# Head means of the first block's keys and queries: one fp32 multiplication, or two one-pass multiplications of a rounded part and a rest

## The chip, the cores and the metric

The kernel runs on one core of a Trainium2 chip. The metric is the device time of one execution in microseconds (us). Three runs of the kernel before took 2369.74 to 2370.86 us, with a median of 2370.79 us.

## The reference

The reference is a chain of two transformer blocks on 256 tokens of width 1024, each of depth 2, in float32. The first block also has 256 context tokens. In the second layer of the first block the context is only read, so queries there cover 256 columns and keys 512. Only one small step matters here. In the first block, queries and keys of two attention families (`na` with a neighbourhood window, `gqa` with grouped heads) are divided by their root mean square over each head of 64 features before they are used:

```
def rms_norm(x, gain=None):
    xf = x.astype(jnp.float32)
    y = xf * lax.rsqrt(jnp.mean(xf * xf, axis=-1, keepdims=True) + EPS)
...
na_q = lambda p: rms_norm(heads(p['na_q'], N_NA_HEADS, HEAD_DIM), na_q_norm)
na_k = lambda p: rms_norm(heads(p['na_k'], N_NA_HEADS, HEAD_DIM), na_k_norm)
gqa_q = lambda p: rms_norm(heads(p['gqa_q'], N_GQA_HEADS, HEAD_DIM), gqa_q_norm)
gqa_k = lambda p: rms_norm(heads(p['gqa_k'], N_GQA_KV_HEADS, HEAD_DIM), gqa_k_norm)
```

The same norm stands behind the gated linear attention (`gla`).

## The kernel before, in words

Activations are kept transposed: 128 features on the partitions, tokens on the free dimension (512 columns for both streams, 256 for the tokens alone). All weights stream from HBM in units of 128 x 1024. ScalarE (ACT) copies each unit, rounded to fp32r, into `ring_high` (L1390), VectorE (DVE) subtracts that from the unit and leaves the rest in `ring_low` (L1920), and TensorE (PE) multiplies in three one-pass products, high by high, high by low and low by high (L816 to L818). A unit is 8 chunks of three such products.

The mixing stage of a layer of the first block runs over steps k = 0 to 20, and each engine has its own written-out program for a step. Between engines there is nothing but semaphores: an engine executes its queue in order, and a wait holds up everything behind it.

- PE in step k: the scores of the attention tile that is due (L1140), pairs of the gated linear attention (L1192), the projection k (24 products, L816 to L818), then the head means that are due (`head_mean`, L1119), then transposes and attention values (L1079, L1158, L1170). Projections 0 to 3 are computed together beforehand; the means of items 0 and 1 are placed inside projection 4, after its fourth chunk, and the products for the gates (L1256) after its sixth.
- ACT in step k: copies of turned tiles (L1648), `qk_square` (L1591), the gates' exponentials (L1663, L1666), the decays (L1714), exponentials of scores (L1616, L1617), copies out of the projection (L1578) and the next unit's high part (L1390), then the root of the mean (`head_root`, L1397 and L1400).
- DVE in step k, in this order: the row maxima of the next attention tile (`maxima`, L2297 to L2316), the scaling by the root (`qk_norm`, L2243), rotary parts, low parts of attention results (L2350), in steps 4 to 6 the gates (`gla_log_gates` L2362 and L2365, `gla_sums` L2371 and L2380), from step 10 four masked copies (L2435), and then `project`: the copy out of projection k (L2218), normalised probabilities (L2334 to L2346) and the low part of a weight unit (L1920).

There are seven normed items in each layer: `NAK`, `NAQ`, `NAK+1`, `NAQ+1`, `GQAK`, `GQAQ`, `GQAQ+1`, numbered i = 0 to 6. Their means fall into steps 2, 2, 5, 7, 9, 10 and 12 (`means_at`). For each, ACT squares the 128 x n item into `squares` (two buffers), PE multiplies the squares by a constant 128 x 128 matrix that holds 1/64 in the two diagonal blocks (`C_ONES64`), ACT makes the reciprocal root and DVE scales the item. n is 512 for all items of the first layer and for the three keys of the second, and 256 for the four queries of the second. The multiplication is a plain fp32 one, which appears as two records in the trace. The gated linear attention has two more such means in each layer, at the end of the mixing.

Of the kernel before, what the change touches and what calls it, by code (L numbers as in the profile page):

```python
# [29 lines left out]
F32 = mybir.dt.float32  # L30
F32R = mybir.dt.float32r
I32 = mybir.dt.int32
ALU = mybir.AluOpType
# [3 lines left out]
P = 128  # L37
# [182 lines left out]
def build(nc, A, old=None):  # L220
    ev = Events(*(old or (None, None)))
    ctx = ExitStack()
    with ctx:
        top = [nc.sbuf_base + (-nc.sbuf_base) % 64]

        def sb(name, cols, dt=F32, over=None):

            if over is None:
                over = top[0] = -(-top[0] // 64) * 64
                top[0] += cols * mybir.dt.size(dt)  # L230
            place_of[name] = over
            return nc.alloc_sbuf_tensor_at(name, [P, cols], dt, offset=over)[:, :]
# [19 lines left out]
        def when(name, *key):  # L252

            if ev.counting:
                return high_parts, 1
            family, value = ev.known[(name, *key)]
            if family not in ev.sems:
                ev.sems[family] = sem(family)
            return ev.sems[family], value
# [59 lines left out]
        wgate = sb("wgate", DEPTH * 2 * P).rearrange("p (l n) -> p l n", l=DEPTH)  # L319
        squares = sb("squares", 2 * N1).rearrange("p (b n) -> p b n", b=2)  # L320
        sumsq = sb("sumsq", N1)
        rstd = sb("rstd", 2 * N1).rearrange("p (b n) -> p b n", b=2)
        act_out = sb("act_out", 2 * N1).rearrange("p (b n) -> p b n", b=2)
        c_wide = act_out[:, 0, 0:KC * 32].rearrange("p (c n) -> p c n", c=KC)
        fresh = sb("fresh", 2 * N1).rearrange("p (b n) -> p b n", b=2)
        zeros = fresh[:, 1, NX:N1]
        narrow = sb("narrow", N2 + 8 * NARROW)
        row_scale = narrow[:, 0:N2]
        gate_w = narrow[:, 16:16 + 16 * NARROW].rearrange("p (s b n) -> p s b n", s=2, b=8)
# [39 lines left out]
        def cst(at, n=P, rows=P):  # L369
            return const[0:rows, at:at + n]  # L370
# [412 lines left out]
        def _(pe):  # L783
# [3 lines left out]
            def take(*key):  # L787

                b = taken[0] % 8
                taken[0] += 1  # L790
                if b in bank_user:
                    pe.wait_ge(*when("free", *bank_user[b]))
                bank_user[b] = key
                ev.banks[key] = b
                return psum[b]
# [319 lines left out]
                mm.then_inc(*made("dft_l", l, s))  # L1115

            def head_mean(tag, i, n):
                pe.wait_ge(*when("head_squares", tag, i))
                pe.matmul(take("head_mean", tag, i)[:, 0:n], cst(C_ONES64),  # L1119
                          squares[:, i % 2, 0:n], start=True, stop=True).then_inc(*made("head_mean", tag, i))  # L1120

            def scores(pr, j):
                q0, nq, nk = pr["tiles"][j]
# [250 lines left out]
        def _(act):  # L1374
# [212 lines left out]
            def head_square(tag, i, ready, x, n):  # L1587
                act.wait_ge(*ready)
                if i >= 2:
                    act.wait_ge(*when("head_mean", tag, i - 2))  # L1590
                act.activation(squares[:, i % 2, 0:n], x, ACT.Square).then_inc(*made("head_squares", tag, i))  # L1591
# [8 lines left out]
            def qk_square(l, i):  # L1600
                tm, (slot, _, n) = ("mix1", l), norm_items(l)[i]
                head_square(tm, i, when("projected", tm, SLOT1[slot]), proj1[:, slot, 0:n], n)

            def exps(pr, j):
                q0, nq, nk = pr["tiles"][j]
# [303 lines left out]
        def _(dve):  # L1909
# [336 lines left out]
            def qk_norm(l, i):  # L2246
                slot, gain, n = norm_items(l)[i]
                head_norm(("mix1", l), i, proj1[:, slot, 0:n], scalar1(l, gain), n, "projected", ("mix1", l),
                          SLOT1[slot])

            def rope_sin(tag, i, sin, n):
                dve.wait_ge(*when("rotated", tag, i))
                if i >= 1:
                    dve.wait_ge(*when("roped", tag, i - 1))
                dve.tensor_tensor(fresh[:, 0, 0:n], bank("rotated", tag, i)[:, 0:n], sin, ALU.mult).then_inc(
                    *made("rope_sin", tag, i, frees=("rotated", tag, i)))
# [149 lines left out]
            def mixing(l):  # L2406
                tm, to = ("mix1", l), ("out1", l)
                n = N1 if l == 0 else NX
                ntile = n // P
                turns = first_tiles(l)  # L2410
                for k in range(MIX_STEPS):
                    if k + 1 in turns:
                        maxima(*turns[k + 1])
                    for i in means_at(l, k - 1):
                        if i not in root_first(l, k - 1):
                            qk_norm(l, i)
                    for i in means_at(l, k - 2):
                        if i >= 4:
                            rope(tm, i - 4, proj1[:, rope_items[i - 4], 0:NX], cst(C_COS1, NX), NX, "head_normed", tm, i)
                    for pr in owed_at(l, k - 1):  # L2420
                        mixed_low(pr)
                    if k == 4:
                        gla_log_gates(l)
                    if k == 5:
                        gla_sums(l, 0)
                    if k == 6:
                        gla_sums(l, 1)
                    if LEVEL_STEP + 1 <= k < LEVEL_STEP + LEVELS + 1:
                        v = k - LEVEL_STEP - 1
                        dve.wait_ge(*when("masks_loaded", 0))  # L2430
                        for h in range(4):
                            dve.wait_ge(*when("pairs", l, v, h))
                            p = bank("pairs", l, v, h)
                            dve.wait_ge(*(when("gla_scores", l, v - 1, h) if v else when("gla_first", l, h)))
                            dve.copy_predicated(gla_s[:, h, 0:ntile], masks[:, v:v + 1].broadcast_to([P, ntile, P]),  # L2435
                                                p[:, 0:n].rearrange("p (t n) -> p t n", n=P)).then_inc(
                                                    *made("gla_scores", l, v, h, frees=("pairs", l, v, h)))
                    if k < len(PROJ1):
                        project(tm, PROJ1, k, width1(l, PROJ1[k]), proj1, VTEMP1, turns.get(k + 1),
                                items=root_first(l, k), rotated=[i for i in means_at(l, k - 1) if i >= 4])  # L2440
                    elif k + 1 in turns:
                        normalise(*turns[k + 1])
                    if k == 6:
                        gla_z(l)
                    if k == LEVEL_STEP - 1:
                        gla_ends(l)
                    if k == LEVEL_STEP + LEVELS:
                        gla_starts(l)
                    s = k - LEVEL_STEP - LEVELS - 3
                    if 0 <= s < 2 - l:  # L2450
                        for c in range(2):
                            dve.wait_ge(*when("gla_out", l, s, c))
                            dve.tensor_copy(proj1[:, GLAQ + c, s * NX:(s + 1) * NX],
                                            bank("gla_out", l, s, c)[:, 0:NX]).then_inc(
                                                *made("gla_out_sb", l, s, c, frees=("gla_out", l, s, c)))
                    if k == len(PROJ1):
                        for s in range(2 - l):
                            dve.wait_ge(*when("dft_d", l, s, 0))
                            dve.tensor_copy(dft_ab[:, s, 0], bank("dft_d", l, s, 0)[:, 0:2 * P]).then_inc(
                                *made("dft_ab_dve", l, s, frees=("dft_d", l, s, 0)))  # L2460
                    if k == len(PROJ1) + 1:
                        hi, lo = x_parts(N1)
                        for s in range(2 - l):
                            if s == 1:
                                gla_finish(l)
                            at = slice(s * NX, (s + 1) * NX)
                            dve.wait_ge(*when("four_high", l, s))
                            dve.tensor_tensor(lo[:, 0:2, at], bank("dft_l", l, s).rearrange("p (g n) -> p g n", g=2),
                                              hi[:, 0:2, at].bitcast(F32), ALU.subtract).then_inc(
                                                  *made("four_low", l, s, frees=("dft_l", l, s)))  # L2470
                        for c in range(2):
                            ev.table[("x_low", to, c)] = ev.table[("four_low", l, 1 - l)]
                for pr in owed_at(l, MIX_STEPS - 1):
                    mixed_low(pr)
# [170 lines left out]
            for c in range(1, KC):  # L2645
# [3 lines left out]
                if c == 1:  # L2649
                    split_ahead(1)  # L2650
            split_ahead(1)
            for l in range(DEPTH):
                for name in ("naq", "gqaq"):
                    dve.tensor_scalar(scalar1(l, name), scalar1(l, name), HD ** -0.5, None, ALU.mult).then_inc(
                        *made("gain_scaled", l, name))
# [168 lines left out]
```

## Time and profile before

| what | value |
|---|---|
| median of 3 runs | 2370.79 us |
| profiled execution | 2369.99 us, span 2368.2 us |
| PE busy | 2348.6 us, 99% of the span |
| DVE, ACT, POOL busy | 65%, 43%, 17% |
| granted TensorE clock, mean | 0.999 |
| mixing, first layer | about 410 to 572 us |
| mixing, second layer | about 1359 to 1479 us |

The profiled execution is 1.8 us longer than its span and 0.8 us shorter than the median. Busy shares say which engine is nearly always at work, but matmuls overlap in the records (the next starts before the end of the last), so what one costs is read from the distance of starts. What a wait costs is read from the stretch in which it lies.

### The profile page before, as it was taken

The page shows a single profiled execution, that of the slowest core. Times are in us where ns is not written, and L with a number is a line of the kernel's source. Part 1 is how long each engine was busy: PE and PEld are TensorE (multiplying, and loading weights), DVE is VectorE, ACT ScalarE, POOL GpSimd, SP SyncE. Part 2 cuts the span into 40 slices and gives each one's busy share as a digit, 9 for nine tenths or more (in the row PEclk, how much of TensorE's full clock was granted, in tenths as well). Part 3 has the DMA queues.
Part 4 walks back from the last instruction along what each step waited for, and adds up shares of the span by engine and source line. Part 5 has one row for each costly group of instructions (what it writes and reads, how often), then busy time and mean ns, then how long its engine had stood idle before and what let it go on. Part 6 is the DMA issues. An engine that isn't in the chain of part 4 may idle for free.

```text
span 2368.2 us, 36508 instructions
## 1 busy us (share of the span) xinstructions
PE 2348.6 (99%) x14378; PEld 2039.4 (86%) x14378; DVE 1534.2 (65%) x2611; ACT 1017.9 (43%) x1734; POOL 405.8 (17%) x427
## 2 busy tenths in 40 slices
PE   9999999999999999999999999999999999999998
PEld 6888889777888888988888877999989999999887
DVE  5888775784698865523322576766677665667874
ACT  5222234654522223422223465545456444456663
POOL 2221221240122131111011121121000220000110
PEclk9999999999999999999999999999999999999999
DMA  9565542212366755222222222555534555434553
GB/s 355 195 209 206 182 159 89 66 55 98 114 212 238 247 207 178 89 98 98 98 94 95 81 99 82 173 184 187 172 118 142 173 175 176 156 120 162 190 188 134
DMA packets 97865, 360.76 MB, mean 152 GB/s; under 512 B 11024, under 2 KB 11792, under 8 KB 96544
## 3 DMA queue, kind: packets, MB, share of 16 engines
q1 hardware_dynamic: 75744, 272.84, 34.3%
q0 software_dynamic: 21952, 85.59, 10.1%
q8 instruction: 115, 1.88, 0.3%
q14 instruction: 54, 0.44, 0.1%
HBM read 357.34 MB, written 1.05 MB: 151 GB/s over the span
## 4 chain that ended last, share of the span: by engine, by line
PE 95%; DVE 1%; ACT 1%; issue 1%; DMA 1%; POOL 0%; DVEq 0%; ACTq 0%; POOLq 0%
PE bank L816 26%; PE bank L818 26%; PE bank L817 26%; PE bank L823 6%; PE bank L824 3%; PE bank L1170 1%; PE bank L1140 1%; PE bank L1158 1%; PE bank L1192 1%; DMA arena<-w_mod_first_dram 1%; PE bank L1119 0%; PE bank L1079 0%; ACT ring_high L1390 0%; PE bank L1344 0%; PE bank L1334 0%
## 5 line engine op out<-in xcount | busy, mean ns | idle before, releaser
L1920 DVE TENSOR_TENSOR ring_low<-ring,ring_high 128x1024 fp32r<-128x1024 f32 x520 | 641.1, 1233 | 484.4 <-ACT ring_high L1390 482.4
L816 PE MATMUL bank<-x_parts,ring_high 128*128 128x512 f32 (+2 forms) x2308 | 799.2, 346 | 2.3 <-POOL x_parts L637 1.4
L1390 ACT ACTIVATE ring_high<-ring 128x1024 fp32r<-128x1024 f32 x520 | 547.9, 1054 | 572.8 <-PE bank L818 528.8
L818 PE MATMUL bank<-x_parts,ring_low 128*128 128x512 f32 (+2 forms) x2308 | 786.3, 341 | 0.0
L817 PE MATMUL bank<-x_parts,ring_high 128*128 128x512 f32 (+2 forms) x2308 | 784.9, 340 | 0.0
L816 PEld LDWEIGHTS bank<-x_parts,ring_high 128*128 128x128 f32 x2308 | 434.6, 188 | 68.0 <-issue 13.2
L818 PEld LDWEIGHTS bank<-x_parts,ring_low 128*128 128x128 f32 x2308 | 434.6, 188 | 47.5
L817 PEld LDWEIGHTS bank<-x_parts,ring_high 128*128 128x128 f32 x2308 | 435.1, 189 | 46.9 <-issue 1.0
L647 POOL TENSOR_TENSOR hidden_parts<-fresh,hidden_parts 128x512 fp32r<-128x512 f32 (+2 forms) x132 | 203.4, 1541 | 1006.2 <-ACT hidden_parts L1523 1006.2
L1933 DVE CUSTOM_DVE_ANT_0 mod_products<-mod_ring,csilu 128x1024 bf16<-128x1024 f32 x224 | 303.1, 1388 | 30.3 <-DMA mod_ring<-w_mod_dram 28.7
L816 PE MATMUL bank<-hidden_parts,ring_high 128*128 128x512 f32 (+2 forms) x814 | 280.9, 345 | 0.2 <-POOL hidden_parts L647 0.2
L818 PE MATMUL bank<-hidden_parts,ring_low 128*128 128x512 f32 (+2 forms) x814 | 280.1, 344 | 0.0
L817 PE MATMUL bank<-hidden_parts,ring_high 128*128 128x512 f32 (+2 forms) x814 | 280.1, 344 | 0.0
L816 PEld LDWEIGHTS bank<-hidden_parts,ring_high 128*128 128x128 f32 x814 | 153.6, 189 | 18.8 <-POOL hidden_parts L647 0.6
L817 PEld LDWEIGHTS bank<-hidden_parts,ring_high 128*128 128x128 f32 x814 | 153.6, 189 | 18.2
L818 PEld LDWEIGHTS bank<-hidden_parts,ring_low 128*128 128x128 f32 x814 | 153.5, 189 | 18.0
L1512 ACT ACTIVATE act_out<-bank 128x512 f32<-128x512 f32 x66 | 39.5, 599 | 264.4 <-PE bank L818 260.0
L823 PE MATMUL bank<-x_parts,ring_high 128*128 128x512 f32 x352 | 123.2, 393 | 0.0
L823 PE MATMUL bank<-hidden_parts,ring_high 128*128 128x512 f32 x308 | 106.9, 392 | 0.0
L816 PE MATMUL bank<-early_parts,ring_high 128*128 128x258 f32 x352 | 99.9, 284 | 0.0
L818 PE MATMUL bank<-early_parts,ring_low 128*128 128x258 f32 x352 | 99.3, 282 | 0.0
L817 PE MATMUL bank<-early_parts,ring_high 128*128 128x258 f32 x352 | 99.3, 282 | 0.0
(268 smaller groups left out, 2756.8 us busy)
## 6 DMA issues: line engine op xcount, KB each, us to landing
ring<-stream_dram SPq DMA_DIRECT2D x517, 512.0 KB, 3.4
mod_ring<-w_mod_dram POOLq DMA_DIRECT2D x128, 512.0 KB, 4.4
arena<-w_mod_first_dram POOLq DMA_DIRECT2D x8, 1024.0 KB, 11.7
ring<-stream_dram POOLq DMA_DIRECT2D x3, 512.0 KB, 10.8
arena<-na_bias_dram POOLq DMA_DIRECT2D x2, 768.0 KB, 11.8
mod_ring<-consts_dram POOLq DMA_DIRECT2D x1, 1076.0 KB, 5.3
resid<-x_dram POOLq DMA_DIRECT2D x2, 512.0 KB, 6.0
resid<-ctx_dram POOLq DMA_DIRECT2D x2, 512.0 KB, 7.2
```

Of the source, the lines that this page charges most:

```text
L647: pool.tensor_tensor(lo[:, f], fresh[:, f % 2, 0:n], hi[:, f].bitcast(F32), ALU.subtract).then_inc(*made("hidden_low", tag, h, f))
L816: pe.matmul(out, w[0][:, b], xh, start=start, stop=False)
L817: pe.matmul(out, w[0][:, b], xl, start=False, stop=False)
L818: return pe.matmul(out, w[1][:, b], xh, start=False, stop=stop)
L823: pe.matmul(bank.rearrange("p (k n) -> p k n", k=2), w[0][:, b], both, start=start, stop=False)
L824: return pe.matmul(bank[:, 0:NX], w[1][:, b], high, start=False, stop=stop)
L1140: mm = pe.matmul(out, pr["q"][r, q:q + nq], pr["k"][r, 0:NZ if twin else nk], start=not fox, stop=True, skip_group_check=nq < P)
L1158: mm = pe.transpose(p[0:rows, kt * P:kt * P + nq], probs[0:nq, b, e, kt * P:kt * P + rows], cst(C_IDENT, nq, nq))
L1390: act.activation(high[:, i % SPLIT], ring[:, u % LOADED], ACT.Copy).then_inc(high_parts, 1)
L1512: act.activation(act_out[:, f % 2, 0:n], p[:, 0:n], ACT.Silu).then_inc(*made("silu", tag, h, f, frees=("gate", tag, h, f)))
L1920: dve.tensor_tensor(low[:, u % LOADED], ring[:, u % LOADED], high_f[:, i % SPLIT], ALU.subtract).then_inc(low_parts, 1)
L1933: dve.tensor_tensor_reduce(junk[:, s], mod_ring[:, n % MOD_RING], csilu[:, s], 1.0, 0.0, ALU.mult, ALU.add, mod[:, l, s, j:j + 1]).then_in ...
```

## The change

The two gated means stay as they were. For the seven query and key items of each layer, ACT makes after the square a second pass, a copy rounded to fp32r (`square_high`); DVE subtracts it from the square and leaves the rest, as fp32r, in the place of the square (`squares_low`, a new step `square_low`); PE multiplies both by the constant matrix in fp32r, adding up in one bank, and now waits for `square_low` where it waited for the square. The rounded part lies in the place of `sumsq`, for item 1 in `fresh`. The constant matrix is rewritten once in its place as fp32r at the start (one DVE copy, `ones64`). `square_low` stands on DVE just ahead of `project` in step k, behind everything else of the step.

```
+            def square_low(l, i):
+                tm, n = ("mix1", l), norm_items(l)[i][2]
+                dve.wait_ge(*when("x_high", tm, "head", i))
+                dve.tensor_tensor(squares_low[:, i % 2, 0:n], squares[:, i % 2, 0:n],
+                                  square_high_of(i)[:, 0:n].bitcast(F32), ALU.subtract).then_inc(
+                                      *made("x_low_dve", tm, "head", i))
...
             def qk_square(l, i):
...
+                if i >= 2:
+                    act.wait_ge(*when("head_mean", tm, i - 1 if i > 2 else 0))
+                act.wait_ge(*when("head_squares", tm, i))
+                act.activation(square_high_of(i)[:, 0:n], squares[:, i % 2, 0:n], ACT.Copy).then_inc(
+                    *made("x_high", tm, "head", i))
...
             def head_mean(tag, i, n):
+                if tag[0] == "gla":
...
+                p = take("head_mean", tag, i)
+                pe.wait_ge(*when("ones64"))
+                pe.wait_ge(*when("x_low_dve", tag, "head", i))
+                pe.matmul(p[:, 0:n], ones64, square_high_of(i)[:, 0:n], start=True, stop=False)
+                pe.matmul(p[:, 0:n], ones64, squares_low[:, i % 2, 0:n], start=False, stop=True).then_inc(
+                    *made("head_mean", tag, i))
...
+                    for i in means_at(l, k):
+                        square_low(l, i)
                     if k < len(PROJ1):
                         project(tm, PROJ1, k, width1(l, PROJ1[k]), proj1, VTEMP1, turns.get(k + 1),
...
+            dve.wait_ge(*when("consts_loaded_rest", 0))
+            dve.tensor_copy(ones64, cst(C_ONES64)).then_inc(*made("ones64"))
```

## Rows read from the trace of the kernel before

**Rows 1.** The page: the chain that ended last, shares of the span by engine.
```profile
PE 95%; DVE 1%; ACT 1%; issue 1%; DMA 1%; POOL 0%; DVEq 0%; ACTq 0%; POOLq 0%
```

**Rows 2.** The chain in order of time, 400 to 440 us: start, us, what.
```profile
416.81 1.72 PE bank L1119 x4
418.52 0.23 PE bank L816
```

**Rows 3.** Timeline of PE, second layer, step 7: start us, us, engine, line, operation.
```profile
1389.00 0.28 PE L818 MATMUL bank<-x_parts,ring_low 128*128 128x256 f32 x1
1389.12 0.60 PE L1119 MATMUL bank<-squares,const 128*128 128x256 f32 x2
1389.78 0.39 PE L817 MATMUL bank<-x_parts,ring_high 128*128 128x512 f32 x1
```

**Rows 4.** Timelines of ACT and DVE: durations of passes like the added ones.
```profile
572.37 1.14 ACT L1423 ACTIVATE x_parts<-arena 128x512 fp32r<-128x512 f32 x2
573.57 1.28 DVE L1970 TENSOR_TENSOR x_parts<-arena,x_parts 128x512 fp32r<-128x512 f32 x2
1482.33 0.99 DVE L1970 TENSOR_TENSOR x_parts<-arena,x_parts 128x256 fp32r<-128x256 f32 x2
```

**Rows 5.** Timelines around items 0 and 1, one row of layer one, three of two.
```profile
417.70 0.69 ACT L1397 ACTIVATE rstd<-bank,eps_one 128x512 f32<-128x512 f32 x1 [1.13 <-PE bank L1119]
...
1363.77 0.92 ACT L1591 ACTIVATE squares<-arena 128x512 f32<-128x512 f32 x2
...
1368.95 1.30 DVE L2243 SCALAR_TENSOR_TENSOR arena<-arena,small,rstd 128x512 f32<-128x512 f32 x2
...
1371.56 1.13 PE L1140 MATMUL bank<-arena 64*128 64x512 f32 x4
```

**Rows 6.** Timeline of DVE, first layer, step 5.
```profile
429.78 0.42 DVE L2297 CUSTOM_DVE_ANT_0 arena<-bank,arena 128x256 f32<-128x256 f32 x1
...
432.17 1.27 DVE L2380 TENSOR_TENSOR_SCAN mod_ring<-eps_one,mod_ring 128x256 f32<-128x256 f32 x2
433.36 0.13 DVE L2334 TENSOR_TENSOR softmax_stats<-softmax_stats 128x1 f32<-128x1 f32 x1
```

**Rows 7.** Timelines of ACT and PE, first layer, step 5.
```profile
428.51 0.61 ACT L1591 ACTIVATE squares<-arena 128x512 f32<-128x512 f32 x1
429.57 1.02 PE L1119 MATMUL bank<-squares,const 128*128 128x512 f32 x2
```

**Rows 8.** Timelines of DVE and PE, second layer, step 5 and the waits behind it.
```profile
1378.61 1.13 PE L1119 MATMUL bank<-squares,const 128*128 128x512 f32 x2 [0.24 <-ACT squares L1591]
...
1381.60 1.27 DVE L2380 TENSOR_TENSOR_SCAN mod_ring<-eps_one,mod_ring 128x256 f32<-128x256 f32 x2
1382.79 0.13 DVE L2334 TENSOR_TENSOR softmax_stats<-softmax_stats 128x1 f32<-128x1 f32 x1
...
1383.35 0.66 PE L1079 MATMUL bank<-const,arena 128*128 128x128 f32 x4 [0.75 <-ACT arena L1578]
...
1398.78 1.95 PE L1170 MATMUL bank<-arena 128*64 128x256 f32 x16 [0.99 <-ACT arena L1648]
```

**Rows 9.** Timelines: DVE in steps 12, 7 and 12, PE in step 12.
```profile
491.93 0.69 DVE L2218 TENSOR_SCALAR arena<-bank 128x512 f32<-128x512 f32 x1 [0.37 <-PE bank L818]
...
1391.82 0.40 DVE L2316 TENSOR_SCALAR softmax_stats<-softmax_stats 128x1 f32<-128x1 f32 x2
...
1425.18 1.44 DVE L2435 COPY_PREDICATED gla_scores<-masks,bank 128x256 f32<-128x256 int32 x4
...
1425.39 0.60 PE L1119 MATMUL bank<-squares,const 128*128 128x256 f32 x2
```

**Rows 10.** PE's first records; stretches at the end (length, busy by engine, PEclk, DMA).
```profile
1.19 5.06 PE L914 MATMUL bank<-fresh 128*128 128x256 f32 x11 [1.19 <-DVE fresh L2592]
...
2357.00:2359.00 2.00, 1.77 (x15) 1.57 (x14) 0.19 (x1) 0.00 (x0) 0.00 (x0) 1.00 0.00 0
...
2361.00:2362.00 1.00, 0.00 (x0) 0.00 (x0) 0.11 (x1) 0.82 (x2) 0.00 (x0) 0.73 0.00 0
```

More of the change, by code:

```diff
@@ L321, in build @@
         sumsq = sb("sumsq", N1)
+        squares_low = sb("squares_low", 2 * N1, F32R, over=place_of["squares"]).rearrange("p (b n) -> p b n", b=2)
+        ones64 = sb("ones64", 2 + P, F32R, over=place_of["const"] + 4 * (C_ONES64 - 2))[:, 2:2 + P]
+        square_high = sb("square_high", N1, F32R, over=place_of["sumsq"])
         rstd = sb("rstd", 2 * N1).rearrange("p (b n) -> p b n", b=2)
@@ L326, in build, with square_high_of @@
         zeros = fresh[:, 1, NX:N1]
+        square_high1 = sb("square_high1", N1, F32R, over=place_of["fresh"] + 4 * N1)
+        def square_high_of(i):
+            return square_high1 if i == 1 else square_high
         narrow = sb("narrow", N2 + 8 * NARROW)
@@ L1117, in head_mean @@
             def head_mean(tag, i, n):
-                pe.wait_ge(*when("head_squares", tag, i))
-                pe.matmul(take("head_mean", tag, i)[:, 0:n], cst(C_ONES64),
-                          squares[:, i % 2, 0:n], start=True, stop=True).then_inc(*made("head_mean", tag, i))
+                if tag[0] == "gla":
+                    pe.wait_ge(*when("head_squares", tag, i))
+                    pe.matmul(take("head_mean", tag, i)[:, 0:n], ones64.bitcast(F32),
+                              squares[:, i % 2, 0:n], start=True, stop=True).then_inc(*made("head_mean", tag, i))
+                    return
+                p = take("head_mean", tag, i)
[4 more added lines that the diff above has]
+                    *made("head_mean", tag, i))
             def scores(pr, j):
```

## The prediction, made before the changed kernel ran

> **What bounds the kernel now.** I read the chain of waits on the page first, then the chain in order of time in the two mixing stages, then the timelines of PE, DVE and ACT there. TensorE carries 95% of the chain [rows 1]: what PE saves in a stage is saved in the time, and what PE waits is lost, unless the stage is one of the few that other engines pace. Inside the first layer's mixing the chain is PE alone; in the second layer, between 1363 and 1399 us, it runs over ACT and DVE, and PE waits for them at the marked places [rows 8]. So the question is how near each of the 14 means stands to the end of its square, now that an ACT pass and a DVE pass come between.
>
> **What PE saves.** Two fp32 means of 512 columns take 1.72 us, so one takes 0.86 [rows 2]. A one-pass product of 512 columns takes 0.23 [rows 2], and the new mean has two: 0.46. Saving 0.40. With 256 columns: from the start of the mean to the second product behind it 0.66 us, less one 0.23 product, is 0.43; a one-pass product of 256 is 0.12 (1389.00 to 1389.12), two are 0.24; saving 0.19 [rows 3]. There are ten means with 512 columns and four with 256: 4.0 + 0.8 = 4.8 us, if PE never waits.
>
> **What is added beside it.** ACT: 14 copies, 0.57 to 0.60 us for 512 columns. DVE: 14 subtractions, 0.64 for 512 columns, and at most 0.5 for 256 (the two in the row have a short wait between them; I take 0.4) [rows 4]. Both read SBUF and write SBUF like the rows they are priced from. The copy at the start, 128 x 128, is below a 128 x 256 pass and DVE idles there; it lies ahead of the first hidden chunk, which waits for PE; I take nothing, at most 0.3 us. The new waits of ACT for earlier means cost nothing: ACT has by then waited for those means in `head_root`.
>
> **Items 0 and 1.** The four ACT passes and two subtractions now stand ahead of the copy out of the gate projection, which ACT waits for before it goes on. In the second layer the squares start at 1363.77 [rows 5]; square, copy, square, copy end at 1365.73, the second subtraction at 1366.15, and everything behind on DVE and ACT is 1.07 us late. PE has its means at about 1365.8, nearly in time, saves 0.6, but its scores of step 5 need item 1 scaled, which ended at 1370.25 [rows 5] and now ends at 1371.3. PE would be there at 1371.0. So 0.25 of the 0.6 us stays. In the first layer ACT had 1.13 us of idle ahead of the root [rows 5], which takes part of the delay: DVE and ACT run some 0.75 us late, item 1 is scaled just in time, and PE keeps 0.8.
>
> **Item 2, the term that decides.** Its subtraction stands in step 5 behind the row maxima and `gla_sums` of that step. In the first layer DVE starts the maxima at 429.78, ends the scans of `gla_sums` at 433.44 and only then comes to `project` (433.36 is its first instruction there) [rows 6]. PE starts the mean at 429.57, just behind the square, which ended at 429.12 [rows 7]. DVE being some 0.75 us late, the subtraction runs from 434.1 to 434.75. PE, 0.8 us early, would start at 428.8 and stands still until 434.8: 6.0 us. In the second layer the scans end at 1382.87 [rows 8]; 1.07 us late, that is 1383.9, and the subtraction is ready at 1384.55. PE was there at 1378.2 (the mean waited 0.24 for its square and started at 1378.61) [rows 8], now at 1377.95: it waits 6.6 us, and the mean ends 5.55 us later than before. Queued behind it on PE is everything of the stage. In the second layer two old waits go, because ACT and DVE catch up meanwhile: about 0.9 us ahead of L1079 (0.75 by the releaser) and 0.99 ahead of L1170 [rows 8]. Bounds for each wait: below, the subtraction as soon as the copy is there (2 us in the first layer); above, one DVE pass of 1.3 us later than I have it.
>
> **The other means.** Second layer, step 7: the maxima end at 1392.22 on DVE [rows 9] and the mean started at 1389.12 [rows 3]. DVE is 1.7 us late by then, PE 4.6: wait 0.6 us. Second layer, step 12: the masked copies ended at 1426.62, the mean started at 1425.39 [rows 9], so the subtraction is ready at 1427.0: wait 1.6 us. DVE is here in step with PE, whose scores it waited for, so a late PE doesn't help. First layer, step 12: DVE had 0.37 us to spare [rows 9] and now needs 0.65: 0.5 us with the semaphore. The rest (steps 7, 9 and 10 of the first layer, 9 and 10 of the second) have DVE in front of PE by more than the pass, and PE simply gains.
>
> **Sum at full clock.** First layer: -0.8 + (6.0 - 0.4) - 3 x 0.4 + (0.5 - 0.4) = +3.7. Second layer: +5.55 (with items 0 and 1 in it), -0.9, +0.6 - 0.2, -1.0, -0.4, -0.2, +1.6 - 0.2 = +4.85. Together +8.5 us.
>
> **The clock.** A wait of 6 us is longer than any inside the kernel before. At its end PE stops its dense products about 2358.8, does two short matmuls, and the granted clock, 1.00 until then, averages 0.73 in the microsecond from 2361 [rows 10]: it went from 2.4 to 1.2 GHz less than 3 us after the products stopped. At the start, PE's first eleven fp32 records of 256 columns begin at 1.19 and 5.06 us hold them, 0.44 apart [rows 10], against 0.43 / 2 = 0.22 for such a record later [rows 3]: PE worked some 4.4 us at the low level before it rose. Half of that time, 2.2 us, is what one fall can cost; nothing is the other end, as shorter waits inside the kernel show no fall. I take 1.8 for each of the two waits, nearer the upper end because the row at the end shows the fall; the 0.6 us wait of step 7 in the second layer then goes. That is +3.0, and +11.5 in all.
>
> The Trainium skill ("TensorE: Matmul & The Clock Gate", "HAM oscillation — how this bites in real kernels") says that a matmul loop that lets the array idle while it waits finds the half clock when it goes on, and pays for the ramp at each such wait. The end of this trace agrees (0.73 in the microsecond from 2361); by the rule both waits pay, without it the sum would stay at +8.5.
>
> From the profiled execution's 2369.99 us this gives 2381.5. The median lies 0.8 higher, so I forecast 2382 us.
>
> **Rivals.**
> - *The clock holds.* For it: nothing inside the kernel before fell. Against: no wait there was this long, and the end of the trace fell sooner. 2370.8 + 8.5 = 2379 us.
> - *Longer low clock, or later waits that I hold for hidden* (steps 7 and 9, where DVE is ahead by about a microsecond): both falls at 2.2 us and two waits of 1 us more give 2385.
> - *The subtraction is in time* (the other side). If DVE came to step 5's subtraction 5 us earlier than the rows show, PE would save its 4.8 us, less the waits of steps 7 and 12 (2.7) and the 0.4 lost at items 0 and 1: 2369, no slower than before. For it speaks only that DVE idles elsewhere in the stage; against it that maxima and scans stand ahead of the subtraction in DVE's order and end 3.9 and 4.3 us after PE's start of the mean. It decides once the two waits of step 5 together are below 4 us.
> - *The one-pass means aren't cheaper*: 4.8 us of saving missing, 2386.5. Against it: the 0.23 and 0.12 us products in the rows are of this type.
>
> **How the numbers follow.** The forecast with the clock falling 0.58, the clock holding 0.2, the longer case 0.13, in time 0.05, no cheaper means 0.04. The bounds of the item 2 waits (2 to 7.5 us) and of the clock (0 to 2.2 each) and the neighbours give 2375 to 2387 us. About 0.2%, 4.7 us, is what a measurement of this kernel can tell from no change. Slower by more, above 2375.5: all cases but the one in time and a small part of the holding clock, 0.93. Within: 0.04. Faster, only if nearly all waits vanish: 0.03.
>
> **What would show it.** Right: the means of item 2 (fifth step of each layer) appear in PE's timeline with idle of about 6 us ahead of them, released by the new DVE subtraction; that subtraction directly behind the scans of `gla_sums`; the idle of 0.75 and 0.99 us ahead of L1079 and L1170 in the second layer gone; a mean pair in 0.46 us where it took 0.86; the granted clock below 1 in the microseconds behind the two waits. Wrong: PE without such idle and a time under 2371 (then DVE's order isn't what holds it), idle of 2 to 3 us (then the copy, not the queue, sets it), or a clock of 1.00 throughout.

## The result: 16 us slower, and the profile after

The changed kernel takes 2386.99 us (median of six runs, 2386.26 to 2387.88) against 2370.69 of the kernel before on the same chip: ratio 1.0071, 95% interval [1.0061, 1.0081]. The forecast was 2382, its range ended at 2387: the direction and the two places that it named were right, the size was 5 us short, and a third place was missed. The profiled execution is 2387.45 us, its span 2385.5, the mean granted clock 0.995.

First the page of the kernel after: its chain by engine, which answers to [rows 1], and PE's largest waits (total us, times, longest).

```profile
PE 93%; DVE 3%; ACT 1%; issue 1%; DMA 1%; POOL 0%; DVEq 0%; ACTq 0%; POOLq 0%
```
```profile
PE bank L1134 <- DVE squares_low L2275: 16.6, 5, 6.3
PE bank L838 <- DVE sumsq L1982: 2.0, 2, 1.4
```

Nearly all of the new waiting is one line: PE in front of the first of the two products of a mean, for DVE's subtraction. Five of the 14 means wait. The timeline of PE in the kernel after shows them, and first item 0 of the first layer, which waits for nothing (start us, us, engine, line, operation, idle before and its releaser):

```profile
416.81 0.39 PE L1134 MATMUL bank<-square_high,ones 128*128 128x512 f32 x1
417.04 0.39 PE L1135 MATMUL bank<-squares_low,ones 128*128 128x512 f32 x1
417.27 0.40 PE L1134 MATMUL bank<-square_high,ones 128*128 128x512 f32 x1
...
434.93 0.77 PE L1134 MATMUL bank<-square_high,ones 128*128 128x512 f32 x1 [5.81 <-DVE squares_low L2275]
435.49 0.63 PE L1135 MATMUL bank<-squares_low,ones 128*128 128x512 f32 x1
...
501.21 0.47 PE L1134 MATMUL bank<-square_high,ones 128*128 128x512 f32 x1 [2.47 <-DVE squares_low L2275]
...
1395.30 0.77 PE L1134 MATMUL bank<-square_high,ones 128*128 128x512 f32 x1 [6.31 <-DVE squares_low L2275]
...
1406.81 0.36 PE L1134 MATMUL bank<-square_high,ones 128*128 128x256 f32 x1 [0.52 <-DVE squares_low L2275]
...
1442.82 0.36 PE L1134 MATMUL bank<-square_high,ones 128*128 128x256 f32 x1 [1.46 <-DVE squares_low L2275]
```

The pair of item 0 starts at 416.81 and that of item 1 at 417.27: a mean takes PE 0.46 us, where [rows 2] had 0.86. At 434.93 the two products start 0.56 us apart, not 0.23: they run at the low clock. DVE's order in the first layer's step 5, timeline of the kernel after, against [rows 6]:

```profile
430.53 0.42 DVE L2325 CUSTOM_DVE_ANT_0 arena<-bank,arena 128x256 f32<-128x256 f32 x1
...
432.92 1.27 DVE L2408 TENSOR_TENSOR_SCAN mod_ring<-eps_one,mod_ring 128x256 f32<-128x256 f32 x2
434.11 0.67 DVE L2275 TENSOR_TENSOR squares_low<-squares,square_high 128x512 fp32r<-128x512 f32 x1
```

The copy that the subtraction needs ended on ACT at 430.60, and maxima and scans stand between:

```profile
429.97 0.63 ACT L1622 ACTIVATE square_high<-squares 128x512 fp32r<-128x512 f32 x1
```

Last the clock: stretches of the kernel after behind the two long waits and behind that of step 12 (stretch, length, busy us of PE, PEld, DVE, ACT, POOL, then the granted clock):

```profile
432.00:434.00 2.00, 0.00 (x0) 0.00 (x0) 1.97 (x5) 1.87 (x8) 0.00 (x0) 0.95 0.00 0
434.00:436.00 2.00, 1.07 (x2) 0.50 (x2) 1.86 (x8) 1.55 (x4) 0.00 (x0) 0.50 0.00 0
436.00:438.00 2.00, 2.00 (x5) 0.51 (x4) 1.49 (x2) 1.32 (x2) 0.00 (x0) 0.50 0.00 0
438.00:440.00 2.00, 2.00 (x7) 1.56 (x6) 1.82 (x9) 0.23 (x1) 0.00 (x0) 0.50 0.00 0
440.00:442.00 2.00, 2.00 (x9) 1.66 (x8) 1.97 (x4) 1.77 (x8) 0.00 (x0) 0.84 0.00 0
...
502.00:504.00 2.00, 2.00 (x12) 1.48 (x12) 0.80 (x1) 1.27 (x2) 0.00 (x0) 0.52 0.00 0
504.00:506.00 2.00, 2.00 (x14) 1.01 (x10) 0.00 (x0) 0.00 (x0) 0.00 (x0) 0.63 0.00 0
...
1396.00:1398.00 2.00, 2.00 (x11) 1.90 (x10) 1.89 (x5) 1.32 (x2) 0.00 (x0) 0.50 0.03 8
```

0.50 is the lower of the clock's two levels (1.2 instead of 2.4 GHz). PE is full of work there and does it at half speed, three times; the prediction had two.

Where the 17 us come in, from the starts of the same PE instructions in the two profiles: the first layer begins +0.2 us late, projection 6 behind item 2 +6.5, that projection's end +7.6 (clock). The cheaper means bring this down to +6.9, and behind step 12 it is +10.8 (item 6 and clock). The second layer begins at +10.6; behind item 2 it is +17.1 and behind the low clock +18.2, it falls to +15.8 as old waits go, and step 12 brings it to +17.3.

### The profile page after: what moved, and what is told of

Read it like the earlier page. It is cut to its first block, busy times and chain, and to the rows that moved or that the text cites. A ratio compares the mean times of both kernels' runs of the same rounds, so it can differ in the third digit from the quotient of the medians.

```text
span 2385.5 us, 36547 instructions
## 1 busy us (share of the span) xinstructions
PE 2351.0 (99%) x14378; PEld 2042.5 (86%) x14378; DVE 1539.9 (65%) x2626; ACT 1026.2 (43%) x1748; POOL 404.1 (17%) x427
## 4 chain that ended last, share of the span: by engine, by line
PE 93%; DVE 3%; ACT 1%; issue 1%; DMA 1%; POOL 0%; DVEq 0%; ACTq 0%; POOLq 0%
PE bank L824 26%; PE bank L826 25%; PE bank L825 25%; PE bank L831 6%; PE bank L832 3%; PE bank L1186 1%; PE bank L1156 1%; PE bank L1174 1%; DMA arena<-w_mod_first_dram 1%; PE bank L1208 0%; ACT ring_high L1406 0%; PE bank L1087 0%; PE bank L1360 0%; DVE gla_scores L2463 0%; PE bank L1350 0%
## 5 line engine op out<-in xcount | busy, mean ns | idle before, releaser
L825 PEld LDWEIGHTS bank<-hidden_parts,ring_high 128*128 128x128 f32 x814 | 153.6, 189 | 18.2
```

What stands on the lines that cost most here:

```text
L825: pe.matmul(out, w[0][:, b], xl, start=False, stop=False)
```

## The experiments

Times are medians with their range. The kernel before took 2369.99 to 2370.51 us beside them and 2370.69 beside the change, so differences between runs are good to some 0.7 us. Where it says "by the starts", the starts of the same PE instructions in two profiles are compared over a mixing stage.

**Is the low clock a cost, and how large?** `busy_wait` leaves the waits and fills them with products.

```diff
                 pe.wait_ge(*when("ones64"))
+                for j in range(22 if i == 2 else 0):
+                    pe.matmul(p[:, 0:n], ones64, chunk(x_parts(N1)[0], j % KC)[:, 0:n], start=True, stop=True)
                 pe.wait_ge(*when("x_low_dve", tag, "head", i))
```

> Both waits of PE ahead of item 2's mean stay, but PE spends 22 products of 0.23 us (5.1 us) in each of them, into the bank that the mean then overwrites. If the clock cost what the trace of the changed kernel shows (PE worked 5.7 us at the low level behind the first wait and 4.5 us behind the second, half of each lost: 2.8 and 2.25 us), the clock stays at 1.00 there and the time falls by about 5 us, to 2382. If the waits alone make the loss and the low clock hides in slack, the time stays at 2387.

2383.14 us (2382.78 to 2383.56), 3.85 less. PE's timeline of this kernel, and a stretch that in the changed kernel had a clock of 0.50:

```profile
428.30 5.30 PE L1134 MATMUL bank<-x_parts,ones 128*128 128x512 f32 x22
434.18 0.50 PE L1136 MATMUL bank<-square_high,ones 128*128 128x512 f32 x1 [0.58 <-DVE squares_low L2277]
```
```profile
434.00:436.00 2.00, 1.82 (x7) 0.70 (x7) 1.86 (x8) 1.92 (x3) 0.00 (x0) 1.00 0.00 0
```

Counted from the start of its stage the mean comes only 0.1 us earlier, the clock is 1.00, and the time falls: the low clock is a cost of its own. But the edit removes three falls and not two. The wait of step 12 in the first layer is 2.47 us long here too, and the clock behind it, 0.50 in the change, is 1.00. PE's timeline and a stretch of this kernel:

```profile
497.88 0.47 PE L1136 MATMUL bank<-square_high,ones 128*128 128x512 f32 x1 [2.47 <-DVE squares_low L2277]
```
```profile
499.00:500.00 1.00, 1.00 (x11) 0.69 (x11) 0.47 (x1) 0.94 (x2) 0.00 (x0) 1.00 0.00 0
```

By the starts, the falls cost 2.65 us behind item 2 and 1.65 behind step 12 in the first layer, and 1.7 behind item 2 in the second, where 0.3 us more lay beside the wait of step 7 (0.81 us here, 0.52 in the change): 6.0 us in all. The time falls by less because PE loses some 2 us outside the stages in this profile: 1.1 at a wait of 1.30 us for POOL at 755 us, and 0.8 up to the second layer. No run shows why.

**Why did item 6's subtraction take 2.71 us?** Timelines of DVE and POOL, kernel after, first layer, step 12:

```profile
495.86 2.58 DVE L2463 COPY_PREDICATED gla_scores<-masks,bank 128x512 f32<-128x512 int32 x4
498.35 2.71 DVE L2275 TENSOR_TENSOR squares_low<-squares,square_high 128x512 fp32r<-128x512 f32 x1
```
```profile
498.15 2.36 POOL L688 TENSOR_TENSOR mod_ring<-mod_ring,arena 128x1024 f32<-128x1024 f32 x1 [1.17 <-ACT mod_ring L1735]
```

The same pass took 0.67 at 434.11. POOL's multiply starts 0.2 us before it and ends at 500.51; the subtraction ends 0.55 us after that. `pool_after_low` makes POOL wait at this one place:

```diff
                 pool.wait_ge(*when("decays", l, v))
+                if (l, v) == (0, 4):
+                    pool.wait_ge(*when("x_low_dve", ("mix1", l), "head", 6))
                 pool.tensor_tensor(decays(l, v), decays(l, v), proj1[:, GLAQ:GLAK + 1, 0:n], ALU.mult).then_inc(
```

> In the first layer, step 12, POOL's multiply of that step waits for item 6's subtraction, so that the two no longer run side by side. If the subtraction took 2.71 us because POOL's multiply (2.36 us, begun 0.2 us before it) held it up, it takes 0.65 us here, PE's wait of 2.47 us ahead of item 6's mean falls to some 0.4 us, no low clock follows it, and the time falls by 2.1 us for the wait and 1.7 us for the clock, to 2383. If the subtraction is slow for a reason of its own (its operands, its queue), it stays at 2.7 us, POOL is only later, and the time is 2387 or more.

2383.43 us (2383.30 to 2384.45), 3.55 less. Timelines of DVE, POOL and PE of this kernel:

```profile
498.07 0.65 DVE L2277 TENSOR_TENSOR squares_low<-squares,square_high 128x512 fp32r<-128x512 f32 x1
```
```profile
498.87 2.38 POOL L690 TENSOR_TENSOR mod_ring<-mod_ring,arena 128x1024 f32<-128x1024 f32 x1 [2.17 <-DVE squares_low L2277]
```
```profile
498.88 0.47 PE L1136 MATMUL bank<-square_high,ones 128*128 128x512 f32 x1 [0.41 <-DVE squares_low L2277]
```

The pass is 0.65 us, PE's wait 0.41 instead of 2.47, and the clock stays at 1.00 behind it: 2.06 us of wait and some 1.5 us of clock (1.65 by the starts). (DVE's next large pass, beside POOL's multiply, now takes 2.74 us instead of 1.21, where nothing waits for it.) The Trainium skill ("SBUF — State Buffer", "Who interferes with whom") says that a DVE instruction with two SBUF inputs contends with a GpSimd instruction that reads SBUF, because both need the read side of a port pair that the two engines share, and that such a pair is locked for one of them until it is done. The rows agree: the 0.55 us behind 500.51 are nearly a whole pass (0.65 to 0.67 us alone), begun when POOL ended.

**Do the two sizes explain the whole miss?** `clock_and_pool` has both edits.

> Both single cures together: PE spends 22 products in each wait of item 2, and POOL's multiply of step 12 in the first layer waits for item 6's subtraction. The waits of item 2 themselves stay. If the miss of the prediction is the size of these two terms, the gains add up (3.85 and 3.55 us), 2379.6, which is the sum that the prediction had at full clock (2370.8 and 8.5, 2379.3). If the two gains lie beside the same slack, the time stays above 2381.

2379.81 us (2379.68 to 2379.93), 7.2 less than the change and 9.3 above the kernel before beside it. That this is the sum of the two gains (7.4) is in part luck: the fall behind step 12 is gone in both runs and so is counted twice, and `busy_wait` lost some 2 us elsewhere. By the starts, the two stages together are longer than before by 17.3 us in the change, 11.3 in `busy_wait`, 13.8 in `pool_after_low` and 9.2 with both edits: 6.0 for three falls, 2.1 for the longer wait of step 12, and the rest stands against the 8.5 that the prediction had at full clock.

**Is DVE's order the cause of item 2's waits?** `low_first` moves the subtraction to the head of the step:

```diff
                 for k in range(MIX_STEPS):
+                    for i in means_at(l, k):
+                        square_low(l, i)
                     if k + 1 in turns:
                         maxima(*turns[k + 1])
...
-                    for i in means_at(l, k):
-                        square_low(l, i)
                     if k < len(PROJ1):
```

> Every subtraction stands at the head of its step on DVE, ahead of maxima, scans and masked copies; nothing else differs from the changed kernel. Item 2's mean then waits only for ACT's copy and the subtraction: 2.3 us in the first layer, 2.9 us in the second, and items 3 and 6 hardly wait. At full clock this gives 2371 less 0.5 (first layer) less 0.7 us (second layer), 2370. If a wait of 2.3 to 2.9 us lets the clock fall as the wait of 2.47 us in step 12 did in the changed kernel, two falls of about 2.2 us are added: 2374. If the place in DVE's order does not matter, 2387.

2374.91 us (2373.83 to 2375.47), 12 less than the change and still slower than before: 1.0019 [1.0011, 1.0028]. By the starts, 4.5 us of the 12 come at item 2 of the first layer, 4.3 at its step 12, where PE no longer waits for the subtraction, and 3.1 in the second layer. PE and the clock behind item 2 in the first layer of this kernel:

```profile
431.24 0.47 PE L1134 MATMUL bank<-square_high,ones 128*128 128x512 f32 x1 [2.36 <-DVE squares_low L2275]
```
```profile
432.00:434.00 2.00, 2.00 (x5) 0.51 (x4) 1.97 (x7) 1.40 (x6) 0.00 (x0) 0.50 0.00 0
```

The waits are as expected (2.36 and 2.88 us), and both let the clock fall: the reading with two falls, 2374. So DVE's order makes 3.4 us of each wait of item 2, and the copy and the subtraction themselves make the rest. Item 3 of the second layer, which was to wait hardly at all, waits 1.29 us.

`item2_alone` splits item 2 only (the other means stay fp32 on the square), and `item2_fp32` all but item 2, both with the subtraction where the change has it. The cut shows `item2_alone`; `item2_fp32` has `i == 2` for `i != 2`. The `return` stands ahead of ACT's copy, and DVE's subtraction is left out for the same items:

```diff
-                if tag[0] == "gla":
+                if tag[0] == "gla" or i != 2:
                     pe.wait_ge(*when("head_squares", tag, i))
...
+                if i != 2:
+                    return
```

> Only item 2 is split, in both layers, with its subtraction where the changed kernel has it; the other means are fp32 means on the square. Without the delay of DVE by items 0 and 1 the waits should be 4.7 us (first layer) and 5.2 us (second), both long enough for the clock to fall: first layer 4.7 less 0.4 and 2.5 for the clock, second layer 5.2 less 0.4, 0.24 and 1.9 of old waits, and 2.2 for the clock: 11.7 us, 2382.5. If the effects simply add up, item 2 alone costs what leaving it out gave back, 6.8 us: 2377.

2380.55 us (2379.60 to 2381.77). The waits are 4.45 and 5.23 us, near the 4.7 and 5.2 expected; the time is 2 us below the sum, and the simple addition (2377) is wrong.

> Item 2 alone is as before in both layers: one fp32 mean on the square, no copy and no subtraction. If the subtraction's place in DVE's queue makes item 2's waits, both waits of 6 us and the low clock behind them go. If nothing takes their place the time is 2387 less 8.4 us (first layer: 5.6 of wait less saving, 2.8 of clock) less 6.3 us (second layer: 5.9 and 2.25, less 1.9 of old waits that come back), 2372. I expect that item 3's mean of the second layer, until now covered by the late PE, waits for its own subtraction behind step 7's maxima instead, some 4 us and perhaps a fall of the clock of 2 us: 2376 to 2378. If the queue is not the cause, 2387.

2380.18 us (2377.91 to 2382.22), more than expected. Both 6 us waits are gone. Four waits for a subtraction are left, in PE's timeline of this kernel:

```profile
447.63 0.47 PE L1134 MATMUL bank<-square_high,ones 128*128 128x512 f32 x1 [1.96 <-DVE squares_low L2277]
...
496.00 0.47 PE L1134 MATMUL bank<-square_high,ones 128*128 128x512 f32 x1 [2.44 <-DVE squares_low L2277]
...
1397.42 0.55 PE L1134 MATMUL bank<-square_high,ones 128*128 128x256 f32 x1 [3.43 <-DVE squares_low L2277]
...
1436.01 0.36 PE L1134 MATMUL bank<-square_high,ones 128*128 128x256 f32 x1 [1.50 <-DVE squares_low L2277]
```

Those of item 6 (2.44 and 1.50 us) stood in the change too. Item 3 of the second layer was expected to surface (3.4 us instead of 4, and the clock fell to 0.50 behind it); item 3 of the first, 1.96 us, was not. The long wait of item 2 had covered these two, or most of them (0.52 us in the change).

**Can the wait be filled with real work?** `item2_late` takes `low_first` and issues item 2's mean in the middle of the sixth projection; `item2_late_3` also keeps item 3 of the second layer fp32.

```diff
-                                {KC // 2 - 1: lambda: first_means(l), KC - 3: lambda: gates_in(l)} if k == 4 else None)
+                                {KC // 2 - 1: lambda: first_means(l), KC - 3: lambda: gates_in(l)} if k == 4 else
+                                {KC // 2 - 1: lambda: head_mean(tm, 2, norm_items(l)[2][2])} if k == 6 else None)
                     for i in means_at(l, k) if k > 2 else ():
-                        head_mean(tm, i, norm_items(l)[i][2])
+                        if i != 2:
+                            head_mean(tm, i, norm_items(l)[i][2])
```

> All 14 means split, subtractions at the head of their steps, and PE issues item 2's mean in the middle of the sixth projection, 2.7 us later, behind 12 of its 24 products. PE then has work during the time that ACT's copy and DVE's subtraction take, and the clock should hold: first layer 2.8 us of gain, second layer 0.65 less 1.3 us of wait at item 3, some 2.2 us in all and 2368 to 2369. Rival: item 2's root on ACT comes 3 us later than before, what stands behind it on ACT (exponentials of step 7) and on DVE (its scaling, the scans) is late by as much, and PE waits for these instead: 2372 or more.

2375.46 us (2373.55 to 2377.00): the rival. PE no longer waits for the mean in the first layer, but for the exponentials behind its late root, and the clock falls there. In the second layer it waits 1.44 us for the mean of item 2, 1.78 for ACT and 1.94 for item 3, at full clock. PE's timeline and a stretch of this kernel:

```profile
440.39 1.13 PE L1156 MATMUL bank<-arena 64*128 64x256 f32 x8 [2.64 <-ACT arena L1640]
```
```profile
442.00:444.00 2.00, 2.00 (x6) 1.61 (x5) 1.90 (x6) 2.00 (x4) 1.99 (x4) 0.50 0.00 0
```

> As the kernel with item 2's mean in the middle of the sixth projection, but item 3 of the second layer keeps its fp32 mean: its wait of 1.3 us goes and 0.2 us of saving with it, so 1.1 us less than that kernel, about 2367. If that wait lies beside another wait of PE that ends at the same time, no difference.

2374.41 us (2372.94 to 2375.40): about the 1.1 us expected between the two, though their ranges overlap, and on the wrong base.

**What is a cheaper mean worth when hardly anything waits for a subtraction?** `no_wait_items` is `low_first` with the three means that waited there for a subtraction (item 2 of both layers, item 3 of the second) fp32; `late_items` splits only items 3 to 6 of the first layer and 5 and 6 of the second. The edits are those of `item2_alone` with other items named.

> Subtractions at the head of their steps, and the three means that still waited there (item 2 of both layers, item 3 of the second) as fp32 means on the square: 11 of the 14 means are split and none of these should make PE wait. If what a split saves is 0.40 us per mean of 512 columns and 0.19 per mean of 256, the first layer gains 0.8 + 4 x 0.4 = 2.4 us and the second 0.25 + 0.4 + 2 x 0.2 = 1.05: 2371 less 3.4, 2367.5. If ACT's and DVE's extra passes or the products themselves eat the saving, 2370 to 2371.

2372.24 us (2371.68 to 2372.80), 4.7 more than expected and no faster than before: 1.0010 [1.0001, 1.0019]. PE, earlier by the first two means, waits for item 2's square (0.81 us in the first layer, 1.31 in the second) and 0.56 us for a subtraction, item 3's of the first layer; DVE's subtraction at the head of step 9 in the second layer makes the maxima late:

```profile
1400.87 1.77 DVE L2277 TENSOR_TENSOR squares_low<-squares,square_high 128x512 fp32r<-128x512 f32 x1
1402.56 0.41 DVE L2327 CUSTOM_DVE_ANT_0 arena<-bank,arena 128x256 f32<-128x256 f32 x1
```
```profile
1400.80 1.29 POOL L688 TENSOR_TENSOR mod_ring<-mod_ring,arena 128x512 f32<-128x512 f32 x1 [0.41 <-ACT mod_ring L1737]
```
```profile
1405.26 0.50 PE L1134 MATMUL bank<-square_high,ones 128*128 128x512 f32 x1 [1.02 <-ACT arena L1640]
```

The subtraction lies beside POOL again, the maxima come 2.1 us later than in the kernel before, and PE waits 1.02 us for the exponentials behind them.

> All 14 means are fp32 means on the square as before, there is no subtraction, but ACT still makes its 14 copies, which nothing reads. If the two copies at step 2 make ACT late for item 2's square and the copies of the second layer make it late for the exponentials of step 8, PE waits some 0.5 us more ahead of item 2 and 1 us ahead of item 4 there: 2371.5. If ACT's copies are hidden, 2370.

2370.20 us (2370.09 to 2370.64), with the edits of `item2_alone` on PE and DVE for all items and ACT's copy left in: ACT's 14 copies cost nothing by themselves.

> Split means only where nothing waited: items 3 to 6 of the first layer, 5 and 6 of the second, subtractions at the head of the step. PE saves 4 x 0.4 and 2 x 0.2 us, 2 in all, less 0.8 that came back as waits of steps 8 and 10 in the first layer: 2369, so hardly to be told from before. If the saving comes back in full, 2370; if it stays in full, 2368.

2369.33 us (2369.12 to 2369.55), ratio 0.9995 [0.9986, 1.0004]: as expected, and not to be told from before.

**What is the most that PE could gain?** `one_pass` leaves the low part out.

```diff
-                pe.matmul(p[:, 0:n], ones64, square_high_of(i)[:, 0:n], start=True, stop=False)
                 pe.matmul(p[:, 0:n], ones64, squares_low[:, i % 2, 0:n], start=False, stop=True).then_inc(
...
-                act.activation(squares[:, i % 2, 0:n], x, ACT.Square).then_inc(*made("head_squares", tag, i))
+                out = squares if tag[0] == "gla" else squares_low
+                act.activation(out[:, i % 2, 0:n], x, ACT.Square).then_inc(*made("head_squares", tag, i))
```

(The mean waits for `head_squares`; its one product has start and stop set.)

> ACT writes the square rounded and PE makes one product of it; the part that the rounding drops is left out, so there is no copy, no subtraction and no new wait. A mean of 512 columns then costs PE 0.23 us instead of 0.86, one of 256 columns 0.12 instead of 0.43: 7.5 us less if PE is what holds the two stages, 2363. If ACT and DVE stand close behind PE there (the kernel without item 2's split gained nothing although PE had 11 cheaper means), part comes back as waits for squares, roots and exponentials: some 3 us in the first layer and 1 in the second stay, 2367.

2365.61 us (2364.94 to 2365.82), ratio 0.9979 [0.9970, 0.9988]: faster than both kernels, by 4.9 of the 7.5 us that its products save. PE's waits of this kernel show most of the rest: old ones that have grown, and those for the square, of which [rows 8] had one at 0.24 us.

```profile
PE bank L1134 <- ACT squares_low L1607: 1.4, 2, 1.3
PE bank L1087 <- ACT arena L1593: 1.3, 1, 1.3
PE bank L1185 <- ACT arena L1670: 1.2, 1, 1.2
```

## Why the prediction was right in direction and 5 us short

Two terms of the sum failed. The larger is the wait of step 12 in the first layer, which met POOL's multiply; the smaller is the price of the low clock. The table has the sum's terms, and what the starts show in the profile of the change; the clock's part is the change less `busy_wait`.

| term, us | predicted | by the starts |
|---|---|---|
| first layer: items 0 and 1 | -0.8 | -0.8 |
| item 2 at full clock | +5.6 | +5.6 |
| clock behind it | +1.8 | +2.65 |
| items 3 to 5 | -1.2 | -0.8 |
| item 6 (step 12) at full clock | +0.1 | +2.3 |
| clock behind it | 0 | +1.65 |
| second layer at full clock | +4.85 | +5.0 |
| clock in it | +1.2 | +1.7 |
| sum | +11.5 | +17.3 |

The two profiled executions lie 17.5 us apart, the medians 16.3, so the table explains the profiles and the medians only roughly.

*The saving per mean* held: 0.46 us for a pair, and the pairs at full clock give PE 0.36 to 0.42 us each. That of item 5 in the first layer comes back at once, as a wait of 0.31 us for DVE ahead of L1208.

*Items 0 and 1* went nearly as worked out in the second layer: a wait of 0.23 us for the scaled item 1 ahead of the scores of step 5, and PE enters the stretch up to item 2 0.05 us later than it entered the layer (predicted: 0.25 earlier).

*Item 2* was the term that decides, by the mechanism given. Predicted 6.0 and 6.6 us, measured 5.81 and 6.31; the subtraction predicted for 434.1, measured at 434.11. The old waits of [rows 8] ahead of the turn (0.75) and of the values (0.99) are gone. `low_first` shows that DVE's order makes 3.4 us of each: at the head of the step 2.36 and 2.88 us are left.

*Steps 7 and 12 of the second layer*: predicted 0.6 and 1.6, measured 0.52 and 1.46.

*Step 12 of the first layer* is the term that failed. "DVE had 0.37 us to spare [rows 9] and now needs 0.65: 0.5 us with the semaphore": the wait was 2.47 us, and the clock fell behind it, 3.9 us where the sum had 0.1. The 0.65 was a row of a pass with POOL idle; here the pass stood beside POOL's multiply. With POOL moved away the wait is 0.41, as predicted, and the time 3.55 us lower. The prediction weighs DVE's queue and has no row of POOL in that step. The kernel before shows one, POOL's timeline there:

```profile
491.26 2.37 POOL L680 TENSOR_TENSOR mod_ring<-mod_ring,arena 128x1024 f32<-128x1024 f32 x1 [1.17 <-ACT mod_ring L1714]
```

DVE came free at about 491.55, 0.37 us ahead of the copy at 491.93 [rows 9], so the added pass was bound to start just behind this multiply.

*The clock* was right as a mechanism and too small as a term. "I take 1.8 for each of the two waits", less 0.6, made 3.0; by the starts the two falls of item 2 cost 4.4, and a third, behind step 12, was not in the sum. The 0.6 was the wait of step 7, which was to go: 0.52 us of it stayed. PE worked 5.7 us at the low level behind the first wait, against the 4.4 us read off the start of the kernel [rows 10], of which half is lost: 2.85 at most, above the 2.2 that I took for the upper end. The rival in which the clock holds is out, and so are the subtraction in time and means that aren't cheaper. The measured time alone would fit the last of these (2386.5, and by the prediction's own terms 2370.8 + 11.5 + 4.8 = 2387.1); what rules it out is the pair's 0.46 us. The rival "longer low clock, or later waits" named the right kind of miss, but placed the waits in steps 7 and 9, and its 2385 was too low as well.

What I would have missed next is the value of the saving. The prediction's rival in time counted all of the 4.8 us less known waits; `no_wait_items` and `one_pass` show that in these two stages ACT and DVE stand close behind PE, so that part of whatever PE saves comes back as waits that no row of the kernel before has.

## What to carry to other kernels

A product made cheaper by an extra pass on another engine is worth what it saves only if that pass is queued near its input: here the pass took 0.67 us, and its place behind maxima and scans made 3.4 us of a wait of 6. Even where almost nothing waited, 1.2 us were left of a saving of 2 (`late_items`, not to be told from before). A duration taken from a quiet row must be checked against what POOL does at the place where the pass will run. And a wait of PE is priced with the half clock behind it: the three waits of 2.5 to 6.3 us cost 6.0 us more than their length within the two stages.

## What was not expected of the hardware

A wait need not be long for the clock to fall, and its length alone doesn't decide. Behind waits of 2.36 and 2.88 us (`low_first`), 2.47 (the change) and 2.64 (`item2_late`) the granted clock was 0.50 for a while. Behind 2.47 us in `busy_wait`, and behind 1.96 and 2.44 us in `item2_fp32`, it stayed at 1.00. The last of these:

```profile
494.00:496.00 2.00, 0.00 (x1) 0.03 (x1) 2.00 (x2) 0.65 (x1) 1.30 (x1) 1.00 0.67 233
496.00:498.00 2.00, 2.00 (x16) 1.55 (x18) 1.58 (x2) 1.23 (x2) 0.00 (x0) 1.00 0.07 29
```

All three kernels have this wait at the same place, item 6 of the first layer: 2.47 us cost the clock in the change, and the same 2.47 us did not in `busy_wait`. No run here settles what sets them apart.
